# A two-layer diffusion trunk on one core: the convolution's variance root, the second key scale and a modulation end change places in the first attention

## The chip, the cores and the metric

The kernel runs on one core of one Trainium2 chip. The metric is the device time of one execution in microseconds; of the kernel before there are three runs. The engines named here are TensorE (PE: matmuls and transposes through the array), VectorE (DVE), ScalarE (ACT), GpSimd (POOL) and SyncE (SP, which issues the weight loads).

## What is computed

The reference is a trunk of two layers over 256 latent and 256 context tokens of width 1024. Layer 0 mixes with dense attention (8 heads, 2 key heads, width 128) beside a gated depthwise convolution with a layer norm; layer 1 with banded attention beside a state space scan; each is followed by a SwiGLU. Shifts, scales and gates come from a modulation product of a condition vector with `mod_w`.

```python
def layer_norm(x, g, b):
    mu = jnp.mean(xf, axis=-1, keepdims=True)
    var = jnp.mean(jnp.square(xf - mu), axis=-1, keepdims=True)
    y = (xf - mu) * lax.rsqrt(var + EPS) * g + b

def conv_module(u, dw_w, dw_b, cn_g, cn_b):
    a, gte = jnp.split(u, 2, axis=-1)
    hdn = depthwise_conv(a * jax.nn.sigmoid(gte), dw_w, dw_b)
    return jax.nn.silu(layer_norm(hdn, cn_g, cn_b))

# even_mixer (layer 0)
q = apply_rope(rms_norm(heads(q, 128), q_g), cos, sin)
k = apply_rope(rms_norm(heads(k, 128), k_g), cos, sin)
attn = dense_block_attention(q, concat([kc, k]), concat([vc, v]))
out = concat([attn, conv_module(glu, ...)], axis=-1) @ w_out
```

## The kernel before

Everything is held transposed, features on the 128 partitions and the 512 tokens (256 latent, 256 context) along the row. A weight product is done in three passes: ScalarE copies the loaded weights to a rounded part `w_hi` (L545), VectorE makes the rest `w_lo` (L555), and TensorE adds hi by hi, hi by lo and lo by hi (L1923 to L1925). Weights stream through four raw buffers; SyncE refills one when its split, or for modulation weights its product, is done.

Each engine has its own program in an order written by hand, and they meet at semaphores. Layer 0 runs ten input blocks (`blocksA`; the last one is v), then attention, then eight output blocks (`out_block`), then the feed-forward part.

Attention has 32 units u, unit u being head u // 4 and token tile u % 4. Latent tiles (u % 4 below 2) see all 512 keys, context tiles 256. TensorE computes the scores of u + 2 (`S_`, L2171), in units 0 to 7 a part of a modulation product (`mod_unit`, L1862), turns the probabilities of u (`turn`, transposes at L1810), multiplies those of u − 1 with V (`pv`, L2146), and then does `conv_sums(u)`. VectorE takes the maximum (L1352), the bias of the exponential (L1373), the inverse of the sum (L1367) and scales the probabilities (L1378) in `softmax_step`; then one tap of the convolution (L1267), as long as there are taps. ScalarE does the exponential of u + 1 (`exp`, L779), copies the turned probabilities of u (L801), after every fourth unit the output tile (`out_hi`, L771), and then `conv_squares(u)`. A score bank is used again after three units.

**The query and key scales.** The sums of squares of the queries are collected in `qrow`. `query_roots` turns them on TensorE, ScalarE takes the root `qsc` (L761), VectorE inverts and scales it (L1335, L1336). The keys' inverse roots are spread over the partitions by `spread_key` (L2013) and multiplied in by `scale_key(h)` (L1302); key 1 serves heads 4 to 7, and the P-times-V of u = 4 waits for it, since it writes the same bank.

**The modulation.** A group of modulation products ends with a copy (`mod_copy`), a turn on TensorE (`mod_T`) and `mod_final(n)` on VectorE: two additions of the bias (L1162), for some groups two gains (L1168), and a memset (L1171) that marks `mod_ready`. The next group's first product waits for that mark. MOD_TURN is 8.

**The convolution's layer norm.** From unit 22 on the mean and the variance are summed on TensorE into `pmod`. After unit 29's copies ScalarE takes the root of the variance (L812), VectorE the reciprocal in unit 30 (L1415), and in unit 31 TensorE spreads it over the partitions (`spread_groups`, L2117). Then `out_block(0, 0)` begins, which uses only attention outputs, and after it stands `pv(31)`. VectorE scales the convolution with the spread root (L1422), ScalarE applies the last activation, and VectorE takes its low part (L1425); output block 2 needs these. The third and fourth activation wait for `pv(31)`.

In `product` the argument `upper` is a function that is called once, ahead of the fifth k tile of the first output column, after twelve matmuls; before, it waits there only for the second half of the split weights.

Of the kernel before, what the change touches and what calls it, by code (L numbers as in the profile page):

```python
# [26 lines left out]
P = 128  # L27
# [130 lines left out]
def build_trunk(nc, a, out):  # L158
    with ExitStack() as ctx:
# [151 lines left out]
        def s(name):  # L311
            if name not in S:
                S[name] = sem(name)
            return S[name]
# [333 lines left out]
        def _(act):  # L648
# [154 lines left out]
            def conv_squares(u):  # L803

                for i in {CONV_STATS + 4: (0, 1), CONV_STATS + 6: (2, 3)}.get(u, ()):
                    act.wait_ge(s("yc_ready"), i + 1)
                    if i >= 2:
                        act.wait_ge(s("var_mm"), i - 1)
                    A(yq[:, i % 2, :], yc[:, i, :], ACT.Square).then_inc(s("yq_ready"), 1)
                if u == 29:  # L810
                    act.wait_ge(s("var_mm"), BT)
                    A(l_rt[:, 0, :], pmod[:, 0:P], ACT.Sqrt, scale=1.0 / B_WIDTH, bias=epsc[:, 0:1])\  # L812
                        .then_inc(s("lrt_ready"), 1)
# [75 lines left out]
            w = C_IN  # L889
# [175 lines left out]
        def _(dve):  # L1065
# [86 lines left out]
                                                     in1=vec[:, N2G + KD:N2G + 2 * KD], op0=ALU.add, op1=ALU.mult))  # L1152
                V_.memset(ysum[:, 0:1], 0.0).then_inc(s("mod_ready"), 1)

            def mod_final(n):
                l, j = GROUPS[n]
                dve.wait_ge(s("modT_done"), n + 1)
                for v in range(2):

                    src = pmod[:, :].rearrange("p (b g c) -> p g b c", b=4, g=4)[:, :, :, v]  # L1160
                    b0 = MODB + 48 * l + 16 * j
                    step(V_.tensor_tensor(mod[:, l, 16 * j:16 * j + 16, v].rearrange("p (g b) -> p g b", g=4), src,  # L1162
                                          vec[:, b0:b0 + 16].rearrange("p (g b) -> p g b", g=4), ALU.add))
                norm_of = {0: (2 * l, SC1, N1G), 2: (2 * l + 1, SC2, N2G)}.get(j)
                if norm_of:
                    k, sc, g0 = norm_of
                    for v in range(2):
                        step(V_.scalar_tensor_tensor(out=gain[:, k, :, v], in0=mod[:, l, sc:sc + KD, v], scalar=1.0,  # L1168
                                                     in1=vec[:, g0 + KD * l:g0 + KD * (l + 1)], op0=ALU.add,
                                                     op1=ALU.mult))  # L1170
                V_.memset(ysum[:, 0:1], 0.0).then_inc(s("mod_ready"), 1)  # L1171

            def inverse_root(n, t):

# [160 lines left out]
            step(V_.reciprocal(qsc[:, :, :], qsc[:, :, :]))  # L1335
            V_.tensor_scalar(qsc[:, :, :], qsc[:, :, :], A_HD ** -0.5, None, ALU.mult).then_inc(s("qsc_ready"), 1)  # L1336
            dve.wait_ge(s("qsc_ready"), 1)
            scale_key(1)
            mod_final(1)

            def attention(layer, O_hi, O_lo, pr, nk_of, qcol, at_end, sink=None, between=None):

                n0 = 32 * layer

                def softmax_step(v, u):

                    if v is not None:  # L1350
                        dve.wait_ge(s("s_done"), n0 + v + 1)
                        top = step.mark(V_.reduce_max(sm[:, v % 3, 0:1], sbank[v % 3][:, nk_of(v)[0] * P:T], AX.X))  # L1352
                    if u is not None:
                        dve.wait_ge(s("exp_done"), n0 + u + 1)
                        total = sm[:, u % 3, 2:3]
                        if sink is not None:
                            dve.wait_ge(s("sink_done"), u + 1)
                            total = sm[:, u % 3, 6:7]
                            summed = step.mark(V_.tensor_tensor(total, sm[:, u % 3, 2:3], sm[:, u % 3, 3:4], ALU.add))
                    if v is not None and sink is not None:  # L1360
                        step.need(top)
                        top = step.mark(V_.tensor_scalar(sm[:, v % 3, 5:6], sm[:, v % 3, 0:1], qcol(v), sink(v), ALU.mult,
                                                         ALU.max))
                    if u is not None:
                        if sink is not None:
                            step.need(summed)
                        inverse = step.mark(V_.reciprocal(sm[:, u % 3, 4:5], total))  # L1367
                    if v is not None:
                        step.need(top)
                        if sink is not None:  # L1370
                            ins = V_.tensor_scalar(sm[:, v % 3, 1:2], sm[:, v % 3, 5:6], -1.0, None, ALU.mult)
                        else:
                            ins = V_.tensor_scalar(sm[:, v % 3, 1:2], sm[:, v % 3, 0:1], qcol(v), -1.0, ALU.mult, ALU.mult)  # L1373
                        ins.then_inc(s("nb_ready"), 1)
                    if u is not None:
                        step.need(inverse)
                        p_ = pr[:, u % 3, nk_of(u)[0] * P:T]
                        V_.tensor_scalar(p_, p_, sm[:, u % 3, 4:5], None, ALU.mult).then_inc(s("p_norm"), 1)  # L1378

                def out_lo(tile):  # L1380
                    dve.wait_ge(s("o_hi"), 8 * layer + tile + 1)
                    w = T if layer == 0 else LAT
                    V_.tensor_tensor(O_lo[:, tile, 0:w], po[tile % 2][:, 0:w], O_hi[:, tile, 0:w].bitcast(F32),
                                     ALU.subtract).then_inc(s("o_lo"), 1)

                softmax_step(0, None)
                softmax_step(1, None)
                softmax_step(None, 0)
                for u in range(32):
                    softmax_step(u + 2 if u + 2 < 32 else None, u + 1 if u + 1 < 32 else None)  # L1390
                    if u == MOD_TURN:
                        mod_copy(2)
                    if u - 2 == MOD_TURN:
                        mod_final(2)
                    if layer == 0:
                        conv_taps(1)
                    if u % 4 == 1 and u > 4:
                        out_lo(u // 4 - 1)
                    if between is not None:
                        between(u)  # L1400
                at_end()
                out_lo(7)

            def conv_centre(u):

                if u == CONV_STATS + 1:
                    dve.wait_ge(s("mu_sum"), 1)
                    V_.tensor_copy(l_mu[:, :], pmod[:, 0:P]).then_inc(s("mu_copied"), 1)
                for i in {CONV_STATS + 3: (0, 1), CONV_STATS + 4: (2, 3)}.get(u, ()):
                    dve.wait_ge(s("mu_mm"), 1)  # L1410
                    V_.scalar_tensor_tensor(out=yc[:, i, :], in0=pmod[:, :], scalar=-1.0 / B_WIDTH, in1=Y[:, i, :],
                                            op0=ALU.mult, op1=ALU.add).then_inc(s("yc_ready"), 1)
                if u == 30:
                    dve.wait_ge(s("lrt_ready"), 1)
                    V_.reciprocal(l_rt[:, 1, :], l_rt[:, 0, :]).then_inc(s("lrs_ready"), 1)  # L1415

# [388 lines left out]
        def _(pe):  # L1805
# [3 lines left out]
            def T_(o, x, n=P):  # L1809
                return nc.tensor.transpose(o, x, cst("ident", 0, n, 0, n))  # L1810
# [206 lines left out]
            def auxA(m):  # L2017
# [21 lines left out]
                    ins = mm(ROT_BANK[m % 2][:, i * LAT:(i + 1) * LAT], cst("rotA"), QK[:, 2 * m + i, 0:LAT], start=True, stop=True)  # L2039
                ins.then_inc(s("aux_done"), 1)  # L2040

            for n, (kind, _, _) in enumerate(blocksA):
                lo = 2 * (n % 2)
                if n >= 2:
# [19 lines left out]
                if n == 0:  # L2064
                    mod_unit(7)
                    continue
                ins.then_inc(block_done, 1)
                if 1 <= n <= 8:
                    mod_unit(KD + n - 1)
                if n == 5:  # L2070
# [3 lines left out]
                    auxA(n - 5)  # L2074
                if n >= 8:
                    spread_key(n - 8)

            def query_roots():

                pe.wait_ge(s("qrow_ready"), 1)  # L2080
                pe.wait_ge(s("rope_done"), 4)
                T_(p5[:, 0:P], qrow[:, :]).then_inc(s("qrow_T"), 1)
                pe.wait_ge(s("rope_done"), 5)
                pe.wait_ge(read_dve, after_A_in["dve"])

            pe.wait_ge(s("k_scaled"), 1)

            def conv_sums(u):
# [10 lines left out]
                for i in {CONV_STATS + 5: (0, 1), CONV_STATS + 7: (2, 3)}.get(u, ()):  # L2099
                    pe.wait_ge(s("yc_ready"), BT)  # L2100
                    pe.wait_ge(s("yq_ready"), i + 1)
                    group_sums(yq[:, i % 2, :], i).then_inc(s("var_mm"), 1)
                if u == 31:
                    pe.wait_ge(s("lrs_ready"), 1)
                    spread_groups(l_rt[:, 1, :]).then_inc(s("lrs_spread"), 1)

            def group_sums(x, i):

# [11 lines left out]
            def attention(layer, nk_of, scores, value, pr, prT, out_of):  # L2120
# [27 lines left out]
                    ins.then_inc(s("pv_done"), 1)  # L2148

                S_(0)  # L2150
                query_roots()
                S_(1)
                for u in range(32):
                    if u + 2 < 32:
# [32 lines left out]
            def second_weights(n, w):  # L2187
# [8 lines left out]

                return enter

            def out_block(l, n):

                w, kt, hi, lo, t, reads0, waits, norm = OUT[l]
# [3 lines left out]
                if n in (4, 6):  # L2205
# [3 lines left out]
                second = n in (2, 3, 5, 7)  # L2209
                product([acc[:, 2 * (pair % 2) + m, 0:t] for m in range(2)], w_h, w_l,  # L2210
                        lambda j: (hi[:, kt * part + j, 0:t], lo[:, kt * part + j, 0:t]), kt,
                        first=not second, last=second, apart=n == 7, upper=lambda: part_ready(w + n, 1))\
                    .then_inc(block_done, 1)
                square_sums(norm, n, t)

# [412 lines left out]
```

## Time and profile before

| what | value |
|---|---|
| runs | 1224.19 us median of 3 (1223.82 to 1225.85) |
| profiled execution | span 1221.5 us from the first to the last instruction; no other time of this execution is given, and the median of the runs lies 2.7 us above the span |
| TensorE busy | 1171.0 us, 96% |
| VectorE busy | 712.2 us, 58% |
| ScalarE busy | 492.5 us, 40% |
| chain that ended last | TensorE 85%, VectorE 10%, ScalarE 2% |
| mean granted clock | 0.992 |

A span is measured from the first instruction to the last, so that what is saved on the chain that ended last is saved in both. Busy shares are means over stages with different limits.

### The profile page before, as it was taken

How to read it: one execution, taken by the hardware profiler on the slowest of the kernel's cores; microseconds unless marked ns; L12 is line 12 of the kernel's file. 1: busy time of each engine (PE TensorE's matmuls, PEld its weight loads, DVE VectorE, ACT ScalarE, POOL GpSimd, SP SyncE). 2: the span in 40 equal slices, each digit the busy share in tenths (PEclk: the TensorE clock that was granted, in tenths of full speed). 3: DMA queues.
4: the chain of work that ended last, by engine and by line, in shares of the span. 5: the costliest groups of instructions: out<-in, count | busy, mean ns of one | idle time of the engine just before them, and what ended most of it. 6: DMA issues, size and time to landing. Idle time of an engine off the chain costs nothing.

```text
span 1221.5 us, 18383 instructions
## 1 busy us (share of the span) xinstructions
PE 1171.0 (96%) x7498; PEld 954.3 (78%) x7498; DVE 712.2 (58%) x1185; ACT 492.5 (40%) x741; POOL 27.3 (2%) x31
## 2 busy tenths in 40 slices
PE   4999999999999999999999999999889999999998
PEld 3777776677688888888887668898446798999998
DVE  3499988743542334323333378977979645556544
ACT  4343235742443332222222433455148736554442
POOL 0100000000000000000000000001500000000000
PEclk9999999999999999999999999999999999999999
DMA  9745355016553222433224553434214157546632
GB/s 359 250 153 192 130 177 178 1 61 216 172 173 104 86 69 86 135 106 104 64 63 148 198 185 116 126 108 153 78 44 139 36 173 256 193 133 216 203 111 96
DMA packets 124333, 170.72 MB, mean 140 GB/s; under 512 B 4797, under 2 KB 112743, under 8 KB 120039
## 3 DMA queue, kind: packets, MB, share of 16 engines
q1 hardware_dynamic: 121430, 164.99, 40.3%
q10 hardware_dynamic: 2833, 4.74, 1.3%
q8 instruction: 51, 0.84, 0.3%
q14 instruction: 19, 0.16, 0.0%
HBM read 168.63 MB, written 1.08 MB: 139 GB/s over the span
## 4 chain that ended last, share of the span: by engine, by line
PE 85%; DVE 10%; ACT 2%; issue 2%; DMA 1%; ACTq 0%; SPq 0%; POOL 0%; DVEq 0%
PE acc L1923 22%; PE acc L1924 22%; PE acc L1925 22%; PE pmod L1862 2%; PE acc L1985 1%; PE p L1810 1%; PE acc L1987 1%; PE acc L1986 1%; PE acc L2517 1%; PE p L2543 1%; DVE seg L1714 1%; PE acc L1810 1%; DMA xin<-in_ctx 1%; PE p L2146 1%; DVE sm L1352 1%
## 5 line engine op out<-in xcount | busy, mean ns | idle before, releaser
L555 DVE TENSOR_TENSOR w_lo<-raw,w_hi 128x1024 fp32r<-128x1024 f32 x234 | 259.0, 1148 | 247.6 <-ACT w_hi L545 247.3
L545 ACT ACTIVATE w_hi<-raw 128x1024 fp32r<-128x1024 f32 (+1 forms) x236 | 221.6, 987 | 436.2 <-PE acc L1925 407.0
L1923 PE MATMUL acc<-Hhi,w_hi 128*128 128x512 f32 (+1 forms) x976 | 334.7, 343 | 6.9 <-POOL ptap L624 4.5
L1925 PE MATMUL acc<-Hhi,w_lo 128*128 128x512 f32 (+1 forms) x976 | 332.2, 340 | 0.0
L1924 PE MATMUL acc<-Hlo,w_hi 128*128 128x512 f32 (+1 forms) x976 | 332.1, 340 | 0.0
L1923 PEld LDWEIGHTS acc<-Hhi,w_hi 128*128 128x128 f32 x976 | 186.5, 191 | 32.2 <-issue 9.0
L1925 PEld LDWEIGHTS acc<-Hhi,w_lo 128*128 128x128 f32 x976 | 186.4, 191 | 20.4
L1924 PEld LDWEIGHTS acc<-Hlo,w_hi 128*128 128x128 f32 x976 | 186.5, 191 | 19.9
L1923 PE MATMUL acc<-hid_hi,w_hi 128*128 128x512 f32 (+1 forms) x448 | 157.3, 351 | 0.0
L1924 PE MATMUL acc<-hid_lo,w_hi 128*128 128x512 f32 (+1 forms) x448 | 155.7, 348 | 0.0
L1925 PE MATMUL acc<-hid_hi,w_lo 128*128 128x512 f32 (+1 forms) x448 | 155.7, 348 | 0.0
L1923 PEld LDWEIGHTS acc<-hid_hi,w_hi 128*128 128x128 f32 x448 | 84.9, 190 | 15.2 <-issue 4.8
L1925 PEld LDWEIGHTS acc<-hid_hi,w_lo 128*128 128x128 f32 x448 | 84.8, 189 | 10.9
L1924 PEld LDWEIGHTS acc<-hid_lo,w_hi 128*128 128x128 f32 x448 | 85.0, 190 | 10.3
L1267 DVE SCALAR_TENSOR_TENSOR Y<-U,vec,Y 128x512 f32<-128x512 f32 x120 | 82.3, 747 | 0.2
L1478 DVE TENSOR_TENSOR f_h<-acc,f_gate 128x1024 f32<-128x1024 f32 (+1 forms) x22 | 21.1, 958 | 103.1 <-PE acc L1925 100.5
L1444 DVE SCALAR_TENSOR_TENSOR X<-acc,mod,X 128x256 f32<-128x256 f32 (+1 forms) x72 | 30.7, 478 | 53.9 <-PE acc L1925 53.9
L1985 PE MATMUL acc<-Hhi,w_hi 128*128 128x512 f32 (+1 forms) x96 | 35.4, 369 | 2.6 <-DVE Hlo L1197 2.6
L1923 PE MATMUL acc<-mixC_hi,w_hi 128*128 128x256 f32 x128 | 36.6, 286 | 0.0
L1924 PE MATMUL acc<-mixC_lo,w_hi 128*128 128x256 f32 x128 | 36.2, 283 | 0.0
L1925 PE MATMUL acc<-mixC_hi,w_lo 128*128 128x256 f32 x128 | 36.2, 283 | 0.0
L1862 PE MATMUL pmod<-raw,cvec 128*32 128x512 f32 x256 | 33.2, 602 | 1.2 <-DVE ysum L1171 1.2
(328 smaller groups left out, 1393.3 us busy)
## 6 DMA issues: line engine op xcount, KB each, us to landing
raw<-in_mod_w SPq DMA_DIRECT2D x48, 1024.0 KB, 5.3
raw<-in_ffn_w_in SPq DMA_DIRECT2D x44, 1024.0 KB, 5.1
raw<-in_od_w_in SPq DMA_DIRECT2D x15, 1024.0 KB, 5.3
raw<-in_ffn_w_out SPq DMA_DIRECT2D x16, 768.0 KB, 4.2
raw<-in_ev_w_in SPq DMA_DIRECT2D x10, 1024.0 KB, 7.6
raw<-in_ffn_w_out SPq DMA_DIRECT2D x16, 640.0 KB, 3.8
raw<-in_od_w_out SPq DMA_DIRECT2D x8, 1024.0 KB, 4.9
raw<-in_ev_w_out SPq DMA_DIRECT2D x8, 768.0 KB, 6.0
```

The lines of the kernel that those rows point to most:

```text
L545: nc.scalar.activation(w_hi[:, w % 2, c0:c1], raw[:, r % RAW_SLOTS, c0:c1], ACT.Copy)\
L555: nc.vector.tensor_tensor(w_lo[:, w % 2, c0:c1], raw[:, r % RAW_SLOTS, c0:c1], w_hi[:, w % 2, c0:c1].bitcast(F32), ALU.subtract).then_inc( ...
L1267: ins = V_.scalar_tensor_tensor(out=y, in0=U[:, i, :, tap:tap + LAT], scalar=col, in1=y, op0=ALU.mult, op1=ALU.add)
L1352: top = step.mark(V_.reduce_max(sm[:, v % 3, 0:1], sbank[v % 3][:, nk_of(v)[0] * P:T], AX.X))
L1444: ins = V_.scalar_tensor_tensor(out=xs, in0=acc[:, 2 * pair + i, cols], scalar=gt, in1=xs, op0=ALU.mult, op1=ALU.add)
L1478: V_.tensor_tensor(f_h[:, :, 0:t], acc[:, 2:4, 0:t], f_gate[:, :, 0:t], ALU.mult)\
L1810: return nc.tensor.transpose(o, x, cst("ident", 0, n, 0, n))
L1862: ins = mm(pmod[32 * g:32 * g + 32, :], cvec[:, k, :], raw[:, r % RAW_SLOTS, g * 512:(g + 1) * 512], start=(k == 0), stop=(k == KD - 1))
L1923: mm(outs[m], hi[:, j, cols], xh, start=(first and j == 0), stop=False)
L1924: mm(outs[m], hi[:, j, cols], xl, start=False, stop=False)
L1925: ins = mm(outs[m], lo[:, j, cols], xh, start=False, stop=(last and j == kts - 1))
L1985: mm(o, hi[:, j, cols], xh, start=(j == 0), stop=False)
```

## The change

- ScalarE takes the variance root after unit 30's copy and not after unit 29's; VectorE takes the reciprocal in unit 31 and not in 30.
- TensorE spreads the root inside the first output block, where `upper` is called, and not in unit 31.
- The turn of the query roots comes directly behind block v, ahead of the spread of key 1 and of the first scores. The two waits that stood behind it stay between the first and the second scores.
- On VectorE `scale_key(1)` goes from ahead of the first softmax step to unit 0 of the loop, `mod_final(1)` to behind the maxima of steps 0 and 1.
- `mod_final(2)` is done in four parts in units 10 to 13, and not whole in unit 10. The memset comes with the last.

```diff
 (ScalarE, conv_squares)
-                if u == 29:
+                if u == 30:
                     act.wait_ge(s("var_mm"), BT)
                     A(l_rt[:, 0, :], pmod[:, 0:P], ACT.Sqrt, scale=1.0 / B_WIDTH, bias=epsc[:, 0:1])\
                         .then_inc(s("lrt_ready"), 1)
 (VectorE)
-            def mod_final(n):
+            def mod_final(n, parts=range(4)):
                 l, j = GROUPS[n]
-                dve.wait_ge(s("modT_done"), n + 1)
-                for v in range(2):
+                if 0 in parts:
+                    dve.wait_ge(s("modT_done"), n + 1)
+                for v in [v for v in range(2) if v in parts]:
...
-                    for v in range(2):
+                    for v in [v for v in range(2) if 2 + v in parts]:
...
-                V_.memset(ysum[:, 0:1], 0.0).then_inc(s("mod_ready"), 1)
+                if 3 in parts:
+                    V_.memset(ysum[:, 0:1], 0.0).then_inc(s("mod_ready"), 1)
...
             dve.wait_ge(s("qsc_ready"), 1)
-            scale_key(1)
-            mod_final(1)
...
                 softmax_step(0, None)
                 softmax_step(1, None)
+                mod_final(1)
                 softmax_step(None, 0)
                 for u in range(32):
                     softmax_step(u + 2 if u + 2 < 32 else None, u + 1 if u + 1 < 32 else None)
+                    if u == 0:
+                        scale_key(1)
                     if u == MOD_TURN:
                         mod_copy(2)
-                    if u - 2 == MOD_TURN:
-                        mod_final(2)
+                    if 0 <= u - 2 - MOD_TURN < 4:
+                        mod_final(2, (u - 2 - MOD_TURN,))
...
-                if u == 30:
+                if u == 31:
                     dve.wait_ge(s("lrt_ready"), 1)
                     V_.reciprocal(l_rt[:, 1, :], l_rt[:, 0, :]).then_inc(s("lrs_ready"), 1)
 (TensorE)
+            def query_roots():
+
+                pe.wait_ge(s("qrow_ready"), 1)
+                pe.wait_ge(s("rope_done"), 4)
+                T_(p5[:, 0:P], qrow[:, :]).then_inc(s("qrow_T"), 1)
...
                 ins.then_inc(block_done, 1)
+                if kind == "v":
+                    query_roots()
...
-            def query_roots():
-
-                pe.wait_ge(s("qrow_ready"), 1)
-                pe.wait_ge(s("rope_done"), 4)
-                T_(p5[:, 0:P], qrow[:, :]).then_inc(s("qrow_T"), 1)
-                pe.wait_ge(s("rope_done"), 5)
-                pe.wait_ge(read_dve, after_A_in["dve"])
...
-                if u == 31:
-                    pe.wait_ge(s("lrs_ready"), 1)
-                    spread_groups(l_rt[:, 1, :]).then_inc(s("lrs_spread"), 1)
...
                 S_(0)
-                query_roots()
+                pe.wait_ge(s("rope_done"), 5)
+                pe.wait_ge(read_dve, after_A_in["dve"])
                 S_(1)
...
+            def second_part(l, w, n):
+
+                part_ready(w + n, 1)
+                if l == 0 and n == 0:
+                    pe.wait_ge(s("lrs_ready"), 1)
+                    spread_groups(l_rt[:, 1, :]).then_inc(s("lrs_spread"), 1)
...
-                        first=not second, last=second, apart=n == 7, upper=lambda: part_ready(w + n, 1))\
+                        first=not second, last=second, apart=n == 7, upper=lambda: second_part(l, w, n))\
                     .then_inc(block_done, 1)
```

## Rows read from the trace of the kernel before

**Rows 1.** Windows: stretch, length, busy PE, PEld, DVE, ACT, POOL; granted clock; DMA share, GB/s.
```profile
180.00:196.00 16.00, 16.00 (x109) 7.74 (x109) 11.01 (x31) 6.21 (x16) 0.00 (x0) 1.00 0.95 329
200.00:222.00 22.00, 19.75 (x123) 14.19 (x122) 21.86 (x65) 14.84 (x37) 0.00 (x0) 1.00 0.01 4
240.00:246.00 6.00, 3.08 (x37) 2.50 (x35) 1.71 (x6) 5.94 (x12) 0.00 (x0) 1.00 0.01 3
246.00:250.00 4.00, 3.55 (x16) 3.46 (x17) 2.70 (x5) 2.90 (x5) 0.00 (x0) 0.57 0.00 0
```

**Rows 2.** Chain that ended last, end of attention: start, length, what.
```profile
229.91 0.89 PE pmod L2117 x8
...
242.18 1.28 ACT L812
...
243.86 1.28 ACT L779
...
245.16 0.67 ACT prob L779 x2
...
246.45 0.68 PE acc L1810 x2
247.13 0.85 PE p L2146 x4
247.98 1.71 PE pmod L2117 x8
249.69 0.39 PE acc L1923
...
258.05 0.44 PE p L2146 x4
```

**Rows 3.** Timeline, end of attention: start, length, engine, line, operation, tiles.
```profile
242.10 1.06 PE L2146 MATMUL p<-probT,V 128*128 128x128 f32 x8
...
242.20 0.69 DVE L1383 TENSOR_TENSOR hid_lo<-p,hid_hi 128x512 fp32r<-128x512 f32 x1 [0.42 <-ACT hid_hi L771]
243.48 0.37 ACT L812 ACTIVATE l_rt<-pmod,epsc 128x128 f32<-128x128 f32 x1
...
245.71 0.37 ACT L801 ACTIVATE probT<-acc 128x256 f32<-128x256 f32 x1
...
246.31 0.94 DVE L1415 RECIPROCAL l_rt<-l_rt 128x128 f32<-128x128 f32 x1
...
250.27 2.48 DVE L1422 TENSOR_TENSOR yc<-yc,pmod 128x512 f32<-128x512 f32 x4
...
253.87 0.69 DVE L1425 TENSOR_TENSOR hid_lo<-yz,hid_hi 128x512 fp32r<-128x512 f32 x1 [0.53 <-ACT hid_hi L825]
```

**Rows 4.** Chain that ended last, start of attention.
```profile
169.24 0.89 PE p L2013 x8
...
171.48 0.56 DVE qsc L1335
...
172.30 0.69 DVE QK L1302
...
173.32 0.70 DVE sm L1352
...
175.94 0.66 PE acc L1810 x4
```

**Rows 5.** Timeline, start of attention.
```profile
169.28 1.22 DVE L1333 COPY V<-acc 128x1024 f32<-128x1024 f32 x1
...
172.91 0.38 DVE L1162 TENSOR_TENSOR mod<-pmod,vec 128x16 f32<-128x16 f32 x2
...
173.55 1.06 PE L1862 MATMUL pmod<-raw,cvec 128*32 128x512 f32 x8 [1.16 <-DVE ysum L1171]
```

**Rows 6.** Timeline of VectorE in unit 10, with the tap behind it.
```profile
202.38 0.38 DVE L1162 TENSOR_TENSOR mod<-pmod,vec 128x16 f32<-128x16 f32 x2
...
203.21 0.75 DVE L1267 SCALAR_TENSOR_TENSOR Y<-U,vec,Y 128x512 f32<-128x512 f32 x1
```

## Prediction

> **What bounds the kernel now.** I read the page first. Its line of busy time has TensorE at work for nearly the whole span, so a change pays only where TensorE waits, or where its clock is low. The view of windows over the first attention shows where that is [rows 1]. From 180 to 196 us TensorE is busy throughout, and VectorE for 11.0 of 16 us: TensorE is the bound, with the modulation products between the softmax steps. From 200 to 222 us VectorE is busy for 21.9 of 22 us: it is the bound. From 240 to 246 us TensorE works 3.1 of 6 us, and from 246 to 250 us its granted clock is 0.57 instead of 1.00.
>
> The chain of waits says why [rows 2]. At 242.18 ScalarE loads the table of the root (L812) and at 243.86 the table of the exponential again, for the last softmax step. That exponential starts only at 245.16, and its turn on TensorE (L1810) at 246.45. The last product before it, P times V of step 29, ended at 242.10 + 1.06 = 243.16 [rows 3]. So TensorE idled 3.3 us, and what follows runs at half clock: 0.85 us for four P-times-V matmuls that take 0.44 later and 1.71 us for the spread of eight matmuls that took 0.89 at 229.91 [rows 2]. The first output block starts at 249.69; the P-times-V of step 31 behind it at 258.05.
>
> At the start, block v ends at 169.24, where the spread of the key root begins; that and the first scores stand ahead of the query roots' turn. VectorE begins the query scale behind ScalarE's root at 171.48, scales the second key at 172.30 and adds the modulation at 172.91, and only then takes the first maximum at 173.32 [rows 4, 5]. The first turn is at 175.94.
>
> **The end of attention.** The root moves behind exponential 31. ScalarE is free at 242.18, where the table load stands now, and the scores and the bias of step 31 are long there. So exponential 31 starts at 242.18 and not at 245.16: 2.98 us earlier, and one table load of 1.28 us is gone. From its start to the turn it takes 246.45 − 245.16 = 1.29 us [rows 2], so the turn starts at 243.47. VectorE finishes the low part of tile 6 at 242.20 + 0.69 = 242.89 [rows 3], about when the exponential's sum arrives, which costs 0 to 0.1 us. TensorE is free at 243.16, so it idles 0.3 us and not 3.3. I take it that its clock then stays up. Turn 31 took 0.68 us at half clock, I take 0.3; P times V of step 30 takes 0.44. Its transposed probabilities are copied 0.92 us after the exponential starts (245.71 + 0.37 against 245.16) [rows 2, 3], at 243.10. The output block can start at 243.47 + 0.3 + 0.44 = 244.2, against 249.69.
>
> The spread moves into this block, behind its twelfth matmul. The block runs 8.36 us for 36 matmuls, 0.23 each, the first at half clock 0.39 [rows 2]; so 8.2 us warm, and the twelfth ends near 244.2 + 2.8 = 247.0. **This is the change's new wait**: the rest of the block, and all that TensorE has behind it, now wait for the reciprocal. ScalarE: copy done 243.10, table load 1.28 and root 0.37 [rows 2, 3], done 244.77; reciprocal 0.94 [rows 3], done 245.7. It is 1.3 us early. Behind the root on ScalarE stands the copy of step 31's transpose, at about 245.1; TensorE asks for it only after the block, past 253. The spread costs 0.89 us warm (229.91) and 1.71 cold; between other weights some tenth more, I take 1.0. P times V 31 then starts at 244.2 + 8.2 + 1.0 = 253.4 against 258.05: **4.6 us earlier** (4.0 to 4.9).
>
> The Trainium skill (ScalarE: Activation LUTs, section "What ACT_TABLE_LOAD costs") says that a switch of table sets costs a drain besides the load, 2.66 us in all. The trace has 1.30 us from the load to the root at work, and does not show that drain. By the page an estimate puts the reciprocal at 247.1, just past the twelfth matmul, and the sum would be 0.1 to 0.2 us worse.
>
> Is anything late next? The scaling of the convolution (L1422) starts at 250.27, behind the spread, and the second low part ends at 253.87 + 0.69 [rows 3], 4.3 us after. The spread now ends near 248.0, so this is done by 252.3, before P times V 31; the third activation waits for that product, before and after. All later waits hang on work that moves along. The weights of the second output block are split from about 245.1, some 2 us earlier than now, and wanted at 253.8.
>
> **The start of attention.** The roots' turn goes first, at 169.24. It, the root and the handing over take some 0.5 us (an estimate: 171.48 − 169.24, less 0.89 for the spread and about 0.86 for the scores), so the root is done near 169.7. VectorE copies V until 169.28 + 1.22 = 170.5 [rows 5], and that is what is late next. Reciprocal and scale take from 171.48 to 172.30, 0.8 us [rows 4]: 171.3. The first scores, one short turn later than now, are done before that, at 171.1. The first maximum starts at 171.3 and not at 173.32, 2.0 us earlier, and the exponential's table, 1.28 us behind the root, is there at 171.0. From maximum to turn 0 it takes 175.94 − 173.32 = 2.6 us [rows 4], and the additions put in between take 0.4 (172.91 to 173.32), so the probabilities are ready at 174.3. But two maxima of 0.7 us with their biases of some 0.2 now stand ahead of the additions: these start at 171.3 + 1.8 = 173.1 at the latest, and from their start to the first modulation product it takes 173.55 − 172.91 = 0.64 us [rows 5]. That product stands ahead of turn 0 on TensorE. It starts at 173.6, as it does now, and ends 1.06 us later, at 174.7. So turn 0 comes at 174.7 and not at 175.94: **1.3 us earlier** (0.6 to 1.7), held by the modulation and not by the maximum. The first bound has VectorE's order cost half of the gain, the second has nothing but the probabilities hold the turn.
>
> Moved behind step 0 is the key scale, 0.69 us [rows 4], ahead of a tap. It is not wanted until P times V of step 4; until 196 us VectorE has some 5 of 16 us spare [rows 1], which hides it. Without that cover it would cost its 0.7 us. SyncE's loads of the modulation weights follow the products' marks and shift with them.
>
> **The modulation in parts.** Four operations with the memset, from 202.38 to the tap at 203.21 [rows 6], 0.83 us, now come one in each of steps 10 to 13. VectorE is full there, before and after, so the work moves but does not go: 0. The bounds are −0.8 if all four fall into gaps, which 21.9 of 22 us exclude nearly, and +0.2 for lone short operations that overlap nothing.
>
> **The sum.** 4.6 + 1.3 = 5.9 us on the path, 1221.5 − 5.9 = 1215.6 us of span. The median of the runs is 1224.19, 2.7 us over the profiled span, which I keep: **1218.3 us**.
>
> **The rivals.**
> - Only the end counts. VectorE's longer queue in steps 0 and 1 (key scale 0.69, tap, maximum) delays the next turns until the 1.3 us is eaten. For it speaks that maximum 3 has to wait behind both; against it that TensorE has a modulation product of about 1 us before each turn. 1224.19 − 4.6 = 1219.6.
> - The clock falls at the edge all the same. It fell after an idle time of 3.3 us broken by nothing [rows 1, 2]; now there is 0.3. If it does, the 1.9 us of half clock comes back (0.4 + 0.4 + 0.8 + 0.2): 1220.2.
> - The reciprocal is late. If ScalarE's switch of tables took two loads' time, 1.28 us more [rows 2], the reciprocal would come just at 247.0, at no loss; beyond that each microsecond is one of stall. With 0.3 us beyond: 1218.6. The drain that the Trainium skill names on the page above is of this kind and nearly this size.
> - The spread parts leave the path: 1224.19 − 6.7 = 1217.5.
> - The change does nothing: something unseen, such as the split weights of the output block, holds it until 249. They are in the trace long before; 1224.
> - Slower: the new wait inside the output block. The rest of the block stands behind ScalarE's root and VectorE's reciprocal. If that reciprocal came later than 247.0 + 5.9 = 252.9 it would eat all; 3 us later still, and the kernel takes 1227. It would need a queue of 7 us ahead of it on VectorE or ScalarE, and neither has more than the softmax of step 31.
>
> **Chances.** Forecast 0.78 (its own range 1217.3 to 1219.3), only the end 0.08, clock 0.05, late reciprocal 0.03, parts off the path 0.02, nothing 0.02, slower 0.02. The range from 1217.0 to 1220.2 takes in the cases on both sides and the 0.5 us that a median of runs moves. A measurement tells about 0.2%, 2.4 us, from no change. Faster by more than that: 0.95; within it 0.03; slower 0.02.
>
> **What the profile after must show.** One load of the exponential's table fewer, exponential 31 at once behind the copy of tile 6, a TensorE idle of some 0.3 us and not 3.3 before turn 31, granted clock 1.00 around it, the spread between the matmuls of the first output block with no wait, P times V 31 about 5.9 us earlier than 258.05. At the start turn 0 some 1.3 us earlier, directly behind a modulation product. The forecast is wrong if the clock falls elsewhere, if the spread waits, or if the VectorE-bound stretch is longer than before.

## The result, and the profile after

| | median | runs | ratio to before, 95% interval |
|---|---|---|---|
| before | 1224.01 us | 1223.31 to 1225.85, 4 runs | |
| changed | 1216.83 us | 1215.55 to 1218.51, 4 runs | 0.9945, 0.9933 to 0.9957 |

The ratio is worth 6.7 us of 1224. The changed kernel was measured a second time beside its experiments: 1218.54 us median (1216.06 to 1218.94, 5 runs), before 1223.46, ratio 0.9956, 0.9942 to 0.9970, or 5.4 us. Both intervals lie below 1, so it is faster, by 5 to 7 us by the two ratios; forecast were 5.9. Three single executions stood far above all others (start only 1311.39 us, modulation first 4061.65, one of the kernel before 2329.89): the medians have them in (modulation first is at 1217.52 without its one), the ratios do not. The first median lies 0.2 us below the low end of the range, 1217.0 (the ratio times the 1224.19 that was forecast from gives 1217.5, inside it); where that comes from is told below.

The page of the profiled execution (it took 1215.55 us, 2.2 us more than its span):

```profile
span 1213.4 us, 18386 instructions
...
PE 1166.7 (96%) x7498; PEld 950.2 (78%) x7498; DVE 711.7 (59%) x1185; ACT 490.8 (40%) x740; POOL 27.3 (2%) x31
```

The windows that answer to [rows 1]; columns as there. VectorE is full between 198 and 220 us, as it was between 200 and 222; at the end of attention TensorE is now busy for 5.7 of 6 us, and the clock is 1.00.

```profile
198.00:220.00 22.00, 19.91 (x123) 14.13 (x123) 21.85 (x65) 14.82 (x37) 0.00 (x0) 1.00 0.01 4
238.00:244.00 6.00, 5.69 (x52) 4.76 (x50) 3.01 (x9) 5.97 (x14) 0.00 (x0) 1.00 0.01 3
```

The chain at the end of attention, for [rows 2]:

```profile
241.43 0.44 PE acc L1813 x2
241.87 0.45 PE p L2146 x4
...
245.07 0.89 PE pmod L2117 x8
...
251.41 0.44 PE p L2146 x4
```

Turn 31 and P times V 30 follow the idle time at full clock (0.44 and 0.45 us; they were 0.68 and 0.85), the spread stands between matmuls of the output block at 245.07 with 0.89 us, and P times V 31 is at 251.41 and not at 258.05. The timeline of the same place, for [rows 3]:

```profile
240.07 0.58 ACT L779 ACTIVATE prob<-acc,sm,qsc 128x256 f32<-128x256 f32 x1
240.13 1.06 PE L2146 MATMUL p<-probT,V 128*128 128x128 f32 x8
240.22 0.69 DVE L1383 TENSOR_TENSOR hid_lo<-p,hid_hi 128x512 fp32r<-128x512 f32 x1 [0.42 <-ACT hid_hi L771]
...
240.61 0.40 ACT L801 ACTIVATE probT<-acc 128x256 f32<-128x256 f32 x1
...
241.03 1.28 ACT L812 ACT_TABLE_LOAD   x1
...
242.32 0.37 ACT L812 ACTIVATE l_rt<-pmod,epsc 128x128 f32<-128x128 f32 x1
...
242.72 0.95 DVE L1418 RECIPROCAL l_rt<-l_rt 128x128 f32<-128x128 f32 x1 [1.35 <-ACT l_rt L812]
```

Exponential 31 starts right behind the copy of tile 6, with no table load ahead of it. TensorE waits from 240.13 + 1.06 = 241.19 to 241.43. The reciprocal ends at 242.72 + 0.95 = 243.67, 1.24 us ahead of the spread's first matmul at 244.91.

The timeline at the start, for [rows 4, 5]. The copy of V is the first row; in the kernel before it began at 169.28, so that this execution was 0.57 us early ahead of all that the change touches.

```profile
168.71 1.22 DVE L1335 COPY V<-acc 128x1024 f32<-128x1024 f32 x1
...
170.65 0.69 DVE L1352 TENSOR_REDUCE sm<-acc 128x1 f32<-128x512 f32 x1
...
172.36 0.37 DVE L1163 TENSOR_TENSOR mod<-pmod,vec 128x16 f32<-128x16 f32 x2
...
173.00 1.07 PE L1865 MATMUL pmod<-raw,cvec 128*32 128x512 f32 x8 [1.18 <-DVE ysum L1173]
...
174.00 0.66 PE L1813 MATMUL acc<-const,prob 128*128 128x128 f32 x4
...
174.34 0.68 DVE L1304 TENSOR_TENSOR QK<-QK,p 128x512 f32<-128x512 f32 x1
```

Counted from the copy of V, the first maximum comes at 1.94 us (before 4.04), the first modulation product at 4.29 (before 4.27), turn 0 at 5.29 (before 6.66).

The last of the four parts of the modulation's end with its tap, for [rows 6]: 0.20 us from start to tap, as in the other three.

```profile
206.12 0.16 DVE L1169 SCALAR_TENSOR_TENSOR gain<-mod,vec 128x8 f32<-128x8 f32 x1
206.32 0.75 DVE L1269 SCALAR_TENSOR_TENSOR Y<-U,vec,Y 128x512 f32<-128x512 f32 x1
```

### The profile page after: what moved, and what is told of

Its sections match the earlier page's. It is cut to its first block, busy times and chain, and to the rows that moved or that the text cites. A ratio compares the mean times of both kernels' runs of the same rounds, so it can differ in the third digit from the quotient of the medians.

```text
span 1213.4 us, 18386 instructions
## 1 busy us (share of the span) xinstructions
PE 1166.7 (96%) x7498; PEld 950.2 (78%) x7498; DVE 711.7 (59%) x1185; ACT 490.8 (40%) x740; POOL 27.3 (2%) x31
## 4 chain that ended last, share of the span: by engine, by line
PE 76%; DVE 18%; ACT 2%; DMA 2%; issue 2%; ACTq 0%; SPq 0%; POOL 0%; DVEq 0%
PE acc L1926 20%; PE acc L1928 20%; PE acc L1927 20%; DVE Y L1269 6%; DVE w_lo L555 2%; PE acc L1988 1%; PE p L1813 1%; PE pmod L1865 1%; PE acc L1990 1%; PE acc L1989 1%; PE acc L2525 1%; PE p L2551 1%; PE acc L1813 1%; DVE seg L1717 1%; DMA xin<-in_ctx 1%
```

## The experiments

Times of different executions are compared from the copy of V on, which lies ahead of the change, and at the end of attention from the second sum of the variance (L2110: 241.11 before, 239.14 after), which lies ahead of the moved root. Both stretches are the same within 0.03 us in every trace of the same code, but for the end of start only, told below; whole executions of the changed kernel scatter by 3 us. There are 4 to 12 executions of each altered kernel in a measurement, and one trace. "The ratio says" stands for its share of the kernel before. In the table, "to turn 0" is from the copy of V, "all" from there to P times V 31, "end" from the second variance sum to P times V 31.

| kernel | median | before | ratio, 95% interval | to turn 0 | end | all |
|---|---|---|---|---|---|---|
| before | | | | 6.66 | 16.94 | 88.77 |
| changed | 1216.83 | 1224.01 | 0.9945, 0.9933 to 0.9957 | 5.29 | 12.27 | 82.70 |
| changed, again | 1218.54 | 1223.46 | 0.9956, 0.9942 to 0.9970 | 5.29 | 12.26 | 82.70 |
| end only | 1218.54 | 1223.41 | 0.9961, 0.9948 to 0.9974 | 6.65 | 12.26 | 84.08 |
| start only | 1222.08 | 1223.41 | 0.9989, 0.9981 to 0.9998 | 5.29 | 17.15 | 87.58 |
| root alone | 1221.50 | 1223.41 | 0.9980, 0.9971 to 0.9989 | 6.66 | 15.54 | 87.37 |
| spread alone | 1223.29 | 1223.41 | 0.9998, 0.9989 to 1.0007 | 6.66 | 16.79 | 88.63 |
| filled gap | 1221.36 | 1223.54 | 0.9982, 0.9973 to 0.9991 | 6.67 | 15.56 | 90.30 |
| modulation whole | 1218.54 | 1223.54 | 0.9958, 0.9944 to 0.9973 | 5.29 | 12.28 | 82.74 |
| modulation first | 1217.80 | 1223.54 | 0.9954, 0.9942 to 0.9967 | 4.80 | 12.28 | 82.20 |
| modulation first, again | 1217.97 | 1223.46 | 0.9955, 0.9941 to 0.9968 | 4.80 | 12.28 | 82.24 |
| late turn | 1219.27 | 1223.54 | 0.9965, 0.9952 to 0.9977 | 7.24 | 12.27 | 85.26 |
| late reciprocal | 1219.33 | 1223.46 | 0.9968, 0.9956 to 0.9980 | 5.29 | 14.24 | 84.67 |
| root alone, filled | 1221.23 | 1223.46 | 0.9978, 0.9968 to 0.9987 | 6.67 | 13.97 | 85.82 |

**End only.** The end's edits on the kernel before: the root, the reciprocal and the spread in the block; nothing of the start.

> The kernel before with the end of attention alone changed: root behind the last exponential, reciprocal one unit later, spread inside the first output block. Theory A (two separate gains that add up): against before, P times V of step 31 comes 4.7 us earlier, the time falls by 4.7 us, turn 0 stays where it was, TensorE idles about 0.3 us before turn 31, its clock stays at 1.00. Rival B (the parts lean on each other, the earlier start is needed for part of it): clearly less than 4.7.

The end takes 12.26 us against 16.94, 4.68 less; turn 0 stays at 6.65. The ratio says 4.8 us. Theory A.

**Start only.** The changed kernel with the end put back:

```diff
-                if u == 30:
+                if u == 29:
                     act.wait_ge(s("var_mm"), BT)
...
-                if u == 31:
+                if u == 30:
                     dve.wait_ge(s("lrt_ready"), 1)
...
+                if u == 31:
+                    pe.wait_ge(s("lrs_ready"), 1)
+                    spread_groups(l_rt[:, 1, :]).then_inc(s("lrs_spread"), 1)
```

> The changed kernel with the end of attention put back as before. Theory A: turn 0 is 1.4 us earlier against the same start of the execution, nothing of it is lost until the last units, where TensorE idles 3.3 us and its clock falls as in the kernel before; the time falls by 1.4 us. Rival B (VectorE, which is full from unit 8 to 20, takes the gain back): no change in time.

Turn 0 comes 1.37 us earlier, and from the copy of V to the second variance sum it is 70.43 us against 71.83: the 1.4 us pass whole through the stretch in which VectorE is full. The ratio says 1.3 us. Theory A. The end took 0.2 us more than before: there the half clock began at 246.6 us in the spread and not with turn 31, and ran on into the output block. The two parts' ratios add up to 6.1 us.

**Root alone.** Of the end's edits only the two unit numbers of the root and the reciprocal; the spread stays in unit 31.

> The kernel before with the root behind the last exponential and the reciprocal one unit later, but the spread still in unit 31, ahead of the first output block. Theory A: turn 31 and P times V 30 are 3.0 us earlier as in the changed kernel, then TensorE waits about 1.4 us for the reciprocal (copy, table load, root and reciprocal), and P times V 31 comes 3.3 us earlier than before, so 1.4 us of the 4.7 belong to the place of the spread. Rival B (the new idle time lowers the clock again): only some 1.5 us earlier. Rival C (the root is all of it): 4.7 us.

Turn 31 came as early as in the changed kernel, and the wait for the reciprocal is 1.42 us, as theory A has it. But the end is only 1.40 us shorter and not 3.3, as rival B has it. The timeline and the window:

```profile
243.19 0.61 PE L2146 MATMUL p<-probT,V 128*128 128x128 f32 x4
...
245.21 1.77 PE L2117 MATMUL pmod<-l_rt,const 128*128 128x128 f32 x8 [1.42 <-DVE l_rt L1415]
```
```profile
245.60:249.00 3.40, 3.40 (x13) 2.92 (x13) 3.40 (x6) 2.68 (x4) 0.00 (x0) 0.50 0.27 43
```

The granted clock fell to 0.50 at 245.6, in the spread; the first part of the output block ran at half clock, which is where most of the missing 1.9 us went.

**Root alone, filled.** The same with TensorE's wait filled, to tell the clock from the wait:

```diff
                 if u == 31:
+                    for _ in range(3):
+                        mm(p7[:, 0:256], ident, const[:, 0:256], start=True, stop=True)
                     pe.wait_ge(s("lrs_ready"), 1)
```

> The kernel before with the root behind the last exponential and the spread still in unit 31, as run before, and with three matmuls of constants (256 columns each) in TensorE's wait for the reciprocal. Their result goes to a bank that nobody reads. Theory A (the idle time of 1.4 us beside the shorter one before it is what let the clock fall there): the clock stays at 1.00, and P times V 31 comes 3.3 us earlier than in the kernel before, not 1.4. Rival B (the clock falls there by itself): 1.4 us again.

```profile
244.27 1.46 PE L2105 MATMUL p<-const 128*128 128x256 f32 x6
...
245.85 1.16 PE L2119 MATMUL pmod<-l_rt,const 128*128 128x128 f32 x8
```
```profile
246.00:250.00 4.00, 4.00 (x22) 3.44 (x23) 3.93 (x6) 3.27 (x6) 0.00 (x0) 1.00 0.27 51
```

The trace has two records for each of the three matmuls. The clock stays at 1.00, and the end takes 13.97 us, 2.97 less than before. That the filled wait keeps the clock up fits theory A; of the 3.3 us, 0.3 are missing, the spread taking 1.16 for 0.89 us. But it is one trace each, and the medians of ten runs, 1221.50 and 1221.23, differ by 0.3 us and not by the 1.6 of the ends. Even the two traced executions differ by only 0.6 us in their spans (1219.6 and 1219.0): the filled one came to the copy of V 0.6 us later, and behind attention it has three stretches at half clock, near 800, 899 and 909 us, where root alone has two, near 898 and 908. So the medians can't tell how often the clock falls in either kernel, and what lets it fall behind a wait of this length stays open.

**Spread alone.** Of the end's edits only the spread in the block.

> The kernel before with the spread alone moved into the first output block; the root stays ahead of the last exponential. Theory A: the idle time of 3.3 us and the half clock stay, the spread only changes place, its matmuls then run at full clock but those of the block take their place at half clock: P times V 31 comes 0.1 to 0.8 us earlier, no change that the time can show. Rival C (the place of the spread is what counts): 1.4 us or more.

0.15 us at the end, nothing in the time. Theory A. The place of the spread is worth nothing while the last exponential is late, and 1.4 us of waiting (and a risk for the clock) once it is early.

**Filled gap.**

```diff
                     if layer == 0:
                         conv_sums(u)
+                    if u == 30:
+                        pe.wait_ge(s("exp_done"), 30)
+                        for _ in range(7):
+                            mm(p7[:, 0:256], ident, const[:, 0:256], start=True, stop=True)
```

> The kernel before with seven matmuls of constants (256 columns each) put into TensorE's idle time behind P times V of step 29; their result goes to a bank that nobody reads. Nothing else is moved. Theory A (the idle time is what lowered the clock): the seven take some 3.0 us, turn 31 starts where it did, and turn 31, P times V 30, the spread and the first matmul run at full clock: P times V 31 comes 1.8 us earlier. Rival B (the clock falls here whatever TensorE does): no gain, or a loss where the seven run past the idle time.

```profile
244.00:248.00 4.00, 3.93 (x40) 3.36 (x39) 1.24 (x4) 3.95 (x8) 0.00 (x0) 1.00 0.02 4
248.00:252.00 4.00, 3.73 (x24) 2.99 (x23) 1.68 (x4) 3.15 (x7) 0.00 (x0) 1.00 0.00 0
```
```profile
246.41 3.19 PE L2168 MATMUL p<-const 128*128 128x256 f32 x14
...
249.72 0.95 DVE L1415 RECIPROCAL l_rt<-l_rt 128x128 f32<-128x128 f32 x1
...
249.87 0.44 PE L1810 MATMUL acc<-const,prob 128*128 128x128 f32 x2 [0.27 <-DVE prob L1378]
...
250.72 1.16 PE L2117 MATMUL pmod<-l_rt,const 128*128 128x128 f32 x8
```

Turn 31 takes 0.44 us after the filler and not 0.68, and the clock is 1.00 from 244 to 252 us. The end is 1.38 us shorter, 0.4 less than expected. The turn gave 0.24 us, where 0.38 was reckoned with, and the spread took 1.16 us and not 0.89: with TensorE faster, the reciprocal (done 249.72 + 0.95 = 250.67) became what its first weights wait for. The ratio says 2.2 us. Theory A in direction, the size a little off: matmuls that compute nothing make this kernel faster, because the idle time had lowered the clock. The three traces in which this idle time stands unfilled (before, start only, spread alone) all have the fall of the clock, this one has not. The traced execution is the slowest of the eleven, 1226.61 us, and "all" is longer in it, since the clock fell at the start of attention; see the last section.

**Modulation whole.**

```diff
-                    if 0 <= u - 2 - MOD_TURN < 4:
-                        mod_final(2, (u - 2 - MOD_TURN,))
+                    if u - 2 == MOD_TURN:
+                        mod_final(2)
```

> The changed kernel with the end of the modulation whole in unit 10 again and not in four parts. Theory A (VectorE is full there, so work only moves): the stretch from the first maximum of unit 8's round to the last tap is as long as in the changed kernel within 0.1 us, and so is the time. Rival B (the parts left the path): up to 0.8 us longer. Rival C (lone short operations cost more): up to 0.3 us shorter.

From the copy of V to the second variance sum 70.46 us against 70.43. Theory A: the parts are worth nothing.

**Modulation first.**

```diff
                 softmax_step(0, None)
+                mod_final(1)
                 softmax_step(1, None)
-                mod_final(1)
```

> The changed kernel with the end of the modulation one softmax maximum earlier, behind step 0 and ahead of step 1. Theory A (turn 0 is held by the modulation product ahead of it on TensorE): the product starts 0.8 us earlier, and turn 0 comes 0.3 to 0.6 us earlier, then held by the scaled probabilities of step 0. Rival B (turn 0 is held by VectorE's softmax): turn 0 no earlier, or later by the 0.1 us that is between.

```profile
172.20 1.06 PE L1865 MATMUL pmod<-raw,cvec 128*32 128x512 f32 x8 [0.33 <-DVE ysum L1173]
...
173.55 0.65 PE L1813 MATMUL acc<-const,prob 128*128 128x128 f32 x4 [0.29 <-DVE prob L1378]
```

The product starts 3.45 us behind the copy of V and not 4.29, turn 0 4.80 and not 5.29. Theory A. TensorE now waits 0.29 us for the scaled probabilities, the next in line.

> The changed kernel with the end of the modulation ahead of the maximum of step 1, once more, beside the changed kernel on the same chip. Theory A: turn 0 stands 4.8 us behind the start of the copy of V again and not 5.3, and P times V 31 is 0.5 us earlier; the median is 0.5 us lower, which is less than the runs scatter. Rival B (the 0.5 us is lost on the way): no difference at P times V 31.

Again 4.80, and "all" is 82.24 against 82.70. The medians of the two kernels measured side by side, 1217.97 and 1218.54, are 0.6 us apart and within each other's scatter. It is the version to keep, by the trace and not by the time.

**Late turn.** `query_roots()` back behind `S_(0)`, all else as changed.

> The changed kernel with the turn of the query roots back behind the first scores. Theory A (the early turn and the earlier maximum need each other): the root comes 1.7 us later, VectorE's reciprocal waits for it 1.0 to 1.1 us instead of being held by the copy of V, and turn 0 comes 1.0 us later than in the changed kernel, so that 0.3 to 0.4 of the 1.4 us are left. Rival B (VectorE's order alone brings the gain): turn 0 no later than in the changed kernel.

```profile
170.99 0.55 DVE L1337 RECIPROCAL qsc<-qsc 128x64 f32<-128x64 f32 x1 [0.99 <-ACT qsc L761]
...
174.15 1.93 PE L1865 MATMUL pmod<-raw,cvec 128*32 128x512 f32 x8 [2.25 <-DVE ysum L1173]
...
176.02 1.12 PE L1813 MATMUL acc<-const,prob 128*128 128x128 f32 x4
```
```profile
173.90:177.30 3.40, 3.15 (x13) 1.48 (x14) 2.88 (x9) 0.73 (x3) 0.00 (x0) 0.51 0.21 27
```

VectorE's reciprocal starts 2.21 us behind the copy of V and not 1.14, and the modulation product at 5.37 and not 4.29: 1.1 us later, as theory A has it. Turn 0 came even 0.6 us later than in the kernel before, since here the clock was at 0.51 and the product took 1.93 us. Without that it would be 5.37 + 1.0 = 6.4, an estimate, and the 0.3 us of gain expected.

**Late reciprocal.** The reciprocal behind `split(A_OUT + 1)`, all else as changed.

```diff
-                if u == 31:
-                    dve.wait_ge(s("lrt_ready"), 1)
-                    V_.reciprocal(l_rt[:, 1, :], l_rt[:, 0, :]).then_inc(s("lrs_ready"), 1)
...
                 split(A_OUT + 1)
+                dve.wait_ge(s("lrt_ready"), 1)
+                V_.reciprocal(l_rt[:, 1, :], l_rt[:, 0, :]).then_inc(s("lrs_ready"), 1)
                 dve.wait_ge(s("lrs_spread"), 1)
```

> The changed kernel with VectorE's reciprocal behind its split of the next weights, so that it comes some 3 us later. Theory A (the new wait is real and has a margin of 1.24 us): the reciprocal ends about 1.7 us behind the twelfth matmul, TensorE stalls for that long inside the first output block, and P times V 31 comes 1.7 us later than in the changed kernel. Rival B (TensorE is not held there): no loss. Rival C (the stall also lowers the clock): 1.7 us and up to 1.9 more.

```profile
245.06 0.95 DVE L1421 RECIPROCAL l_rt<-l_rt 128x128 f32<-128x128 f32 x1
...
246.15 1.13 PE L2116 MATMUL pmod<-l_rt,const 128*128 128x128 f32 x8 [1.70 <-DVE l_rt L1421]
```

The stall is 1.70 us, as expected; P times V 31 comes 1.97 us later, the spread behind a stall taking 1.13 and not 0.89 us. The clock did not fall here, behind a longer wait than the 1.42 us of root alone. So the new wait holds TensorE, and the changed kernel stays clear of it by its 1.24 us.

**Changed again.**

> The changed kernel once more, unaltered. Theory A (what its first profiled execution has beyond 6.1 us is the clock elsewhere): from the copy of V to P times V 31 it is as in the first trace within 0.1 us, 6.1 us shorter than before; behind that the trace shows another number of stretches at half clock than the first one, and a span longer by 0.7 to 1.5 us for each stretch more. Rival B (the change also shortens something later): the span is 8 us shorter than before again, with no such difference.

To P times V 31 it is 82.70 us again. Behind that the two executions part. The chain of the first, of the second, and of the kernel before, each at a modulation product and at a product of the second layer's scan:

```profile
703.07 1.85 PE pmod L1865 x16
...
840.87 1.97 PE acc L2460 x4
```
```profile
703.10 1.85 PE pmod L1865 x16
...
842.13 1.97 PE acc L2460 x4
```
```profile
709.72 1.85 PE pmod L1862 x16
...
848.97 1.97 PE acc L2452 x4
```

Up to 703 us both changed executions are 6.6 us ahead of the kernel before. At the second row the first is 8.1 ahead, the second 6.8. The windows say why: first, second, and before.

```profile
794.00:797.40 3.40, 3.00 (x26) 2.93 (x26) 3.33 (x5) 0.00 (x0) 0.00 (x0) 1.00 0.00 0
...
904.00:907.40 3.40, 3.31 (x12) 2.07 (x12) 3.37 (x11) 2.24 (x6) 0.00 (x0) 0.50 0.00 0
```
```profile
795.00:798.40 3.40, 3.02 (x15) 2.94 (x15) 3.33 (x5) 0.00 (x0) 0.00 (x0) 0.50 0.23 26
894.00:897.40 3.40, 3.40 (x26) 2.98 (x27) 1.68 (x4) 0.48 (x2) 0.00 (x0) 0.50 0.00 0
904.20:907.60 3.40, 3.02 (x10) 1.51 (x11) 2.02 (x9) 2.15 (x8) 0.00 (x0) 0.50 0.02 5
```
```profile
802.90:806.30 3.40, 3.40 (x18) 3.40 (x17) 3.33 (x6) 0.00 (x0) 0.00 (x0) 0.50 0.58 155
912.00:915.50 3.50, 3.31 (x12) 2.07 (x12) 3.47 (x11) 2.34 (x7) 0.00 (x0) 0.51 0.00 0
```

Behind attention the first execution has one such stretch at half clock (near 904 us), the second three (795, 894 and 904), the kernel before two (803 and 912); the one at the very end of each trace is left out. The code of the first two is the same, and so is TensorE's busy time ahead of the stretch at 795: 5.00 of 5 us from 785 to 790 and again to 795, in both. The first execution is the exception: the traces of the eleven other experiments have two or three such stretches there. The second one's span is 2.9 us longer, 1.3 by the first extra stretch (842.13 − 840.87, the two executions level before), and the remaining 1.6 I put down to the other. That is theory A, with 1.3 to 1.6 us a stretch.

## Why the prediction was right, point by point

- **Exponential 31 2.98 us earlier, turn 31 soon after.** Right: from the second variance sum to turn 31 it takes 2.29 us and not 5.34, 3.05 less. From exponential 31 to turn 31 it takes 1.36 us (241.43 − 240.07) and not 1.29; the low part of tile 6 stands on the chain there until 240.91, so it cost about 0.07 us, inside the 0 to 0.1 allowed.
- **The clock stays up.** Right here, in all traces with the early exponential and the spread in the block. That the idle time of 3.3 us had lowered it is what filled gap shows. Root alone says that it was no matter of course: there a fall went with an idle time of 1.42 us after one of 0.24, while late reciprocal kept 1.00 through 1.70 us. The length of the idle time alone does not decide it.
- **The new wait is met 1.3 us early.** Right, 1.24; late reciprocal shows it to be a real wait.
- **The drain of the Trainium skill.** ScalarE: Activation LUTs, "What ACT_TABLE_LOAD costs", has a drain of 1.38 us beside the load. In the trace after, the root is at work 1.29 us behind the start of the load (242.32 − 241.03). The drain does not show there, nor in any other trace of this case.
- **Spread in the block 1.0 us.** It cost 0.89. Turn 31 took 0.44 us and not the 0.3 assumed, so two small errors cancel. The end gave 4.67 us for 4.6 forecast: 3.05 by the earlier turn, 1.6 by the clock (0.24 in the turn, 0.40 in P times V 30, 0.82 in the spread, the rest in the block).
- **Turn 0 held by the modulation, 1.3 us earlier.** Right, 1.37; modulation first shows that the product held it. The key scale lies hidden behind step 0 (174.34), the next turns are not later.
- **The working for turn 0.** It is off by little and to its own favour: 173.1 + 0.64 gives 173.74, not 173.6, and 175.94 − 174.7 is 1.24, not 1.3; without rounding the sum is 1.1 us. The additions came at 172.36, 3.65 us behind the copy of V, where the working had 3.8 "at the latest". That the measured 1.37 is so near 1.3 is in part luck.
- **The early turn of the query roots.** Late turn shows the modulation product 1.1 us later without it; that VectorE's order alone is worth 0.3 us is worked out, since the clock fell in that trace.
- **The parts of `mod_final(2)`: 0.** Right, 0.03.
- **The sum.** 5.9 us forecast on the path, 6.07 measured to P times V 31. What was mis-sized is the last step, that everything behind attention takes as long as before. In the first profiled execution it took 1.4 us less, with one stretch at half clock fewer, the one that the kernel before had near 803 us; in the second, which has one stretch more than the kernel before, it took 1.5 us more, 2.9 more than in the first. This makes the range's low end too high for one measurement's median: the 0.5 us that I gave the scatter should have been 1.5. Why one execution has such a stretch and another has not stays open.
- **The clock rival's price.** Its four terms add up to 1.8 us and not 1.9, and by the trace of filled gap the clock is worth 1.4 at this place; the high end of the range rests on the 1.9.
- **The 2.7 us from span to median.** It sets the median of three executions against the span of one of them. Single executions on record take 1.9 to 2.2 us more than their spans. It stands on both sides, before and forecast, so the gain does not hang on it.

## What to carry to other kernels

A table switch between the last two exponentials of an attention costs twice: the switch and back stands on the path, and the idle time that it gives TensorE can lower the clock for the work behind it, here 1.4 us more by the trace of filled gap. Move the odd function behind the last exponential, and put what depends on it inside a long product, at a point behind the one where the function is ready; the trace tells by how much (here 1.24 us). When two waits follow each other, find which engine's next item really holds the release: taking the maximum 2.1 us earlier gave 1.4, because a product that waited for something else stood ahead.

## What the runs showed of the hardware that was not expected

In filled gap the granted clock fell to 0.50 at 175.9 us, in TensorE's wait ahead of turn 0:

```profile
170.00:176.00 6.00, 3.97 (x21) 1.68 (x20) 4.67 (x13) 2.79 (x5) 0.00 (x0) 0.99 0.00 0
176.00:182.60 6.60, 6.15 (x25) 3.84 (x26) 3.63 (x11) 2.81 (x8) 0.00 (x0) 0.50 0.65 199
```

The kernel before has the same code up to there and the same waits (1.16 us ahead of the modulation product, 1.32 ahead of turn 0), and kept 1.00 in its trace. So the fall is not decided by what the engine did alone. In late turn it fell to 0.51 at 173.9 us, in a longer wait, 2.25 us ahead of the modulation product. The changed kernel has 1.18 us ahead of that product and none ahead of turn 0, and neither of its two traces has a fall there.

A few stretches at half clock come and go between executions of one kernel, near 795, 894 and 904 us. In the two traces of the changed kernel they go with 2.9 us of span. Among its first four executions the fastest two, 1215.55 and 1216.34 us, have a mean granted clock of 0.995 and 0.996, the slowest, 1218.51, of 0.992; not every difference follows it. For changes of 0.1% the traces, compared over the stretch in question, told more than medians.
